# Two transformer blocks on one core: how X is turned for a norm without a mean, and when the low part of a row unit is made

## What is computed

```python
for l in range(2):                                # first block
    x = x + gated_parallel_mixer(rmsnorm(x, norm1_g[l]), ...)
    x = x + conv_ffn(rmsnorm(x, norm2_g[l]), ...)
x = rmsnorm(x, final_g)

# second block
x = layer_norm(alpha * x + rwkv_moba_mixer(x), ln1_g[0], ln1_b[0])
x = layer_norm(alpha * x + sq_relu_mlp(x), ln2_g[0], ln2_b[0])
x = layer_norm(alpha * x + dilated_mixer(x), ln1_g[1], ln1_b[1])
x = layer_norm(alpha * x + sq_relu_mlp(x), ln2_g[1], ln2_b[1])

def rmsnorm(x, g):                                # a norm without a mean
    return x * rsqrt(mean(x * x) + 1e-6) * g
```

## Time and profile before

| what | value |
|---|---|
| median of 3 runs | 1582.14 us (1581.43 to 1585.51) |
| the profiled execution, its time | 1585.99 us |
| its span, first to last instruction | 1584.2 us |
| mean granted TensorE clock | 0.997 |
| TensorE busy | 1554.5 us, 98% |
| VectorE busy | 1089.2 us, 69% |
| ScalarE busy | 930.4 us, 59% |
| GpSimd busy | 303.2 us, 19% |
| HBM read | 269.88 MB, 171 GB/s over the span |

### The profile page before, as it was taken

One profiled execution on the slowest core, in us unless ns is written; L12 is line 12 of the kernel. 1 busy time (PEld: TensorE's weight loads), 2 busy tenths in 40 slices (PEclk: granted clock), 3 DMA queues, 4 the chain that ended last, 5 costly groups with the idle time before them and its releaser, 6 DMA issues. The chain is left out here.

```text
span 1584.2 us, 29408 instructions
## 1 busy us (share of the span) xinstructions
PE 1554.5 (98%) x12262; PEld 1424.6 (90%) x12262; DVE 1089.2 (69%) x1702; ACT 930.4 (59%) x1507; POOL 303.2 (19%) x214
## 2 busy tenths in 40 slices
PE   9999999999999999999999999899999999999998
PEld 7999998999899999999988997779988899889986
DVE  5775666887457765668864587679744778789644
ACT  6787756665457776566654664345433666664431
POOL 0000210443000002104420352018500021118300
PEclk9999999999999999999999999999999999999999
DMA  8344455565552534636554631235555535345651
GB/s 331 123 150 144 146 201 186 192 238 197 197 181 92 174 123 157 225 134 213 200 186 173 242 120 55 83 127 193 203 213 196 191 131 187 107 186 192 238 203 59
DMA packets 42324, 272.82 MB, mean 172 GB/s; under 512 B 4816, under 2 KB 4944, under 8 KB 13392
## 3 DMA queue, kind: packets, MB, share of 16 engines
q1 hardware_dynamic: 41184, 265.18, 47.0%
q10 hardware_dynamic: 1008, 5.77, 1.0%
HBM read 269.88 MB, written 1.05 MB: 171 GB/s over the span
## 5 line engine op out<-in xcount | busy, mean ns | idle before, releaser
L330 DVE TENSOR_TENSOR b_wlo<-b_wraw,b_whi 128x2048 fp32r<-128x2048 f32 (+3 forms) x261 | 564.1, 2165 | 178.4 <-PE b_ps L466 126.7
L403 PE MATMUL b_ps<-b_H,b_whi 128*128 128x256 f32 x2152 | 604.8, 281 | 0.5 <-DVE b_trot L796 0.5
L406 PE MATMUL b_ps<-b_H,b_wlo 128*128 128x256 f32 x2152 | 598.1, 278 | 0.0
L405 PE MATMUL b_ps<-b_H,b_whi 128*128 128x256 f32 x2152 | 598.0, 278 | 0.0
L322 ACT ACTIVATE b_whi<-b_wraw 128x2048 fp32r<-128x2048 f32 (+3 forms) x262 | 466.6, 1782 | 205.2 <-PE b_ps L466 149.1
L403 PEld LDWEIGHTS b_ps<-b_H,b_whi 128*128 128x128 f32 x2152 | 404.8, 188 | 8.7 <-issue 6.8
L405 PEld LDWEIGHTS b_ps<-b_H,b_whi 128*128 128x128 f32 x2152 | 406.1, 189 | 0.7
L406 PEld LDWEIGHTS b_ps<-b_H,b_wlo 128*128 128x128 f32 x2152 | 406.0, 189 | 0.0
L1596 POOL TENSOR_TENSOR b_fl<-b_ab,b_fh 128x256 fp32r<-128x256 f32 x44 | 93.8, 2131 | 205.7 <-ACT b_fh L1569 205.7
L1517 POOL TENSOR_TENSOR b_mg<-b_mg,b_scr 128x256 f32<-128x256 f32 x32 | 31.5, 984 | 405.9 <-DVE b_scr L1502 405.9
L463 PE MATMUL b_ps<-b_whi,b_gh 128*128 128x512 f32 x256 | 99.7, 389 | 0.0
(11 more groups left out here) (361 smaller groups left out, 2464.5 us busy)
## 6 DMA issues: line engine op xcount, KB each, us to landing
b_wraw<-in_w SPq DMA_DIRECT2D x221, 1024.0 KB, 4.8
b_wraw<-in_w SPq DMA_DIRECT2D x35, 512.0 KB, 3.4
b_wraw<-in_w SPq DMA_DIRECT2D x6, 768.0 KB, 5.9
b_bias<-in_rpb SPq DMA_DIRECT2D x8, 512.0 KB, 6.4
b_gains<-in_gains ACTq DMA_DIRECT2D x4, 1024.0 KB, 4.8
b_X<-in_x ACTq DMA_DIRECT2D x2, 512.0 KB, 5.4
b_cA<-in_cA SPq DMA_DIRECT2D x2, 512.0 KB, 6.0
out<-b_X SPq DMA_DIRECT2D x4, 256.0 KB, 2.2
```

Of the source, the lines that this page charges most:

```text
L330: e.tensor_tensor(wlo[u % NLO][:, 0:n], raw[u % NRAW][:, 0:n], hi.bitcast(F32), ALU.subtract).then_inc(up("w_lo", "wlo", u))
L403: e.matmul(out, wh, x.hi[:, kk, :], start=k == 0, stop=False)
L405: e.matmul(out, wh, x.lo[:, kk, :], start=False, stop=False)
L406: ins = e.matmul(out, wl, x.hi[:, kk, :], start=False, stop=last)
```

## The change

First, in the four norms without a mean that follow a product (not `n10`, whose kind is now called "first"), the diagonal is no longer made. VectorE writes half 0 of the block of X times `rinv` to a buffer, ScalarE half 1 to a second one, and TensorE transposes these copies with the identity. The buffers are `S_ring[0]` and `S_ring[1]` of the mixer and the two halves of `rows` of the ffn; there is one pair for both token blocks, so block 1's copies wait until block 0's transposes have read them. X stays as it is.

Second, at the last block of every stage end but the final one (seven places), the low part of unit `last + 2` is made by two instructions of 1024 columns, one ahead of the sum into X and one behind it. TensorE's first two k of that unit wait for the first half only, the third k for the second.

The diff, without the places that only hand the buffers on:

```diff
+    def split_lo_in_two(e, w, u, i):
+        a, b = i * UNIT // 2, (i + 1) * UNIT // 2
+        w.wait_ge(*at("whi", u))
+        w.wait_ge(*at("unit", u - NLO))
+        ins = e.tensor_tensor(wlo[u % NLO][:, a:b], raw[u % NRAW][:, a:b], whi[u % NHI][:, a:b].bitcast(F32), ALU.subtract)
+        if i == 0:
+            ins.then_inc(up("w_first_lo", "wlo", "half", u))
+        else:
             ins.then_inc(up("w_lo", "wlo", u))
             w.unit = u + 1
...
-    def row_pe(e, w, job, j, pi, tb, q0=0, q1=None, ring="lin"):
+    def row_pe(e, w, job, j, pi, tb, q0=0, q1=None, ring="lin", in_two=False):
...
-        w.wait_ge(*(at("wlo", u) if u > 1 else at("wlo", "half", u)))
+        in_two = in_two or u < 2
+        w.wait_ge(*(at("wlo", "half", u) if in_two else at("wlo", u)))
         for q in range(q0, q1):
             k = ks[q]
-            if u < 2 and q == 2:
+            if in_two and q == 2:
                 w.wait_ge(*at("wlo", u))
...
             if n == 2 and key != "n10":
-                turn_x_pe(e, w, key, kind, 1)
-            row_pe(e, w, job, *b)
+                turn_x_pe(e, w, key, kind, 1, xs)
+            row_pe(e, w, job, *b, in_two=b[1] == 1)
...
+    def rms_scale_dve(e, w, key, tb, xs):
+        s = tst[:, tb, :]
+        w.wait_ge(*at(key, "root", tb))
+        e.reciprocal(s[:, 4:5], s[:, 3:4]).then_inc(up("x_rinv", key, "rinv", tb))
+        w.wait_ge(*at(key, "rinv", tb))
+        if tb:
+            w.wait_ge(*at("full", ("xt", key, 0, 1)))
+        e.tensor_scalar(xs[0], x_half(0, tb), s[:, 4:5], None, ALU.mult).then_inc(up("x_n", key, "xn", 0, tb))
+
+    def rms_scale_act(e, w, key, tb, xs):
+        w.wait_ge(*at(key, "rinv", tb))
+        if tb:
+            w.wait_ge(*at("full", ("xt", key, 0, 3)))
+        e.activation(xs[1], x_half(1, tb), ACT.Copy, scale=tst[:, tb, 4:5]).then_inc(up("x_n_act", key, "xn", 1, tb))
...
-    def turn_x_pe(e, w, key, kind, tb):
+    def turn_x_pe(e, w, key, kind, tb, xs=None):
...
-                if kind == "rms":
+                if kind == "first":
                     w.wait_ge(*at(key, "diag", tb))
                     ins = e.matmul(out, x, diag[:, tb, :], start=True, stop=True)
                 else:
                     w.wait_ge(*at(key, "xn", f // 4, tb))
-                    ins = e.transpose(out, x, ident)
+                    ins = e.transpose(out, x if xs is None else xs[f // 4][:, f % 4 * P:f % 4 * P + P], ident)
...
             if kind == "rms":
                 rms_sum_act(e, w, key, j, tb, ("free", (job.key, j, tb)))
+                if j == 1:
+                    rms_scale_act(e, w, key, tb, xs)
...
         for n, (j, tb) in enumerate(row_done(job)):
-            ahead_to(e, w, split_lo, begun[(job.key, 0)][-1] + AHEAD_LO if n < 2 and len(begun[(job.key, 0)]) > 1 else last + AHEAD_LO if n == 3 else last - 1 + AHEAD_LO)
+            in_two = n == 3 and kind != "last"
+            ahead_to(e, w, split_lo, begun[(job.key, 0)][-1] + AHEAD_LO if n < 2 and len(begun[(job.key, 0)]) > 1 else last + AHEAD_LO if n == 3 and not in_two else last - 1 + AHEAD_LO)
+            if in_two:
+                split_lo_in_two(e, w, last + AHEAD_LO, 0)
             ahead = kind == "ln" and single(job)
             if not (ahead and (j, tb) == (0, 1)):
                 res_dve(e, w, job, j, tb, scale, need)
+                if in_two:
+                    split_lo_in_two(e, w, last + AHEAD_LO, 1)
                 if kind != "rms":
                     ln_stats_dve(e, w, key, j, tb, ("free", (job.key, j, tb)))
             if j == 1:
                 if kind == "rms":
-                    rms_diag_dve(e, w, key, tb)
+                    rms_scale_dve(e, w, key, tb, xs)
...
+                self.scaled = [S_ring[0][:, :], S_ring[1][:, :]]
...
+                self.scaled = [self.rows[:, 0, :], self.rows[:, 1, :]]
...
         for tb in range(2):
-            turn_x_pe(e, w, "n10", "rms", tb)
+            turn_x_pe(e, w, "n10", "first", tb)
```

More of the change, by code:

```diff
@@ L340, in split_lo_half @@
             w.unit = u + 1
+    def split_lo_in_two(e, w, u, i):
[6 more added lines that the diff above has]
+        else:
+            ins.then_inc(up("w_lo", "wlo", u))
+            w.unit = u + 1
     def half_act(e, w, u, i):
@@ L474, in row_pe, with first_rows_pe @@
             ins.then_inc(up("part", "unit", u))
-    def first_rows_pe(e, w, job, key, kind):
+    def first_rows_pe(e, w, job, key, kind, xs=None):
         blocks = row_blocks(job)
@@ L721, in single, with end_pe @@
         return job.nk <= job.kpart
-    def end_pe(e, w, job, key, kind):
+    def end_pe(e, w, job, key, kind, xs=None):
         blocks = row_blocks(job)
@@ L730, in end_pe, with end_act @@
         if kind != "last":
-            turn_x_pe(e, w, key, kind, 0)
+            turn_x_pe(e, w, key, kind, 0, xs)
         row_pe(e, w, job, *blocks[-1], q)
-    def end_act(e, w, job, key, kind, gkey=None, bkey=None):
+    def end_act(e, w, job, key, kind, gkey=None, bkey=None, xs=None):
         last = last_unit(job)
@@ L747, in end_act, with end_dve @@
                 h_act(e, w, key, gkey, bkey, tb)
-    def end_dve(e, w, job, key, kind, gkey, bkey, scale, need=None):
+    def end_dve(e, w, job, key, kind, gkey, bkey, scale, need=None, xs=None):
         last = last_unit(job)
         for n, (j, tb) in enumerate(row_done(job)):
-            ahead_to(e, w, split_lo, begun[(job.key, 0)][-1] + AHEAD_LO if n < 2 and len(begun[(job.key, 0)]) > 1 else last + AHEAD_LO if n == 3 else last - 1 + AHEAD_LO)
+            in_two = n == 3 and kind != "last"
+            ahead_to(e, w, split_lo, begun[(job.key, 0)][-1] + AHEAD_LO if n < 2 and len(begun[(job.key, 0)]) > 1 else last + AHEAD_LO if n == 3 and not in_two else last - 1 + AHEAD_LO)
+            if in_two:
+                split_lo_in_two(e, w, last + AHEAD_LO, 0)
             ahead = kind == "ln" and single(job)
@@ L1314, in pe @@
             banks.assign(lin=EVERY, att=EVERY)
-            first_rows_pe(e, w, self.v, f"n1{self.l}", "rms")
+            first_rows_pe(e, w, self.v, f"n1{self.l}", "rms", ffns[self.l - 1].scaled if self.l else None)
             for j in range(4):
@@ L1358, in pe @@
                 tile_pe(e, w, self.gates[br] if what == "gate" else self.brs[br], j)
-            end_pe(e, w, self.out, f"n2{self.l}", "rms")
+            end_pe(e, w, self.out, f"n2{self.l}", "rms", self.scaled)
         def act(self, e, w):
@@ L1408, in act @@
                 self.branch_act(e, w, what, *i)
-            end_act(e, w, self.out, f"n2{l}", "rms", f"norm2_g{l}")
+            end_act(e, w, self.out, f"n2{l}", "rms", f"norm2_g{l}", xs=self.scaled)
         def bias_sp(self, e, w, rq):
@@ L1486, in dve @@
                 self.branch_dve(e, w, what, *i)
-            end_dve(e, w, self.out, f"n2{l}", "rms", f"norm2_g{l}", None, 1.0)
+            end_dve(e, w, self.out, f"n2{l}", "rms", f"norm2_g{l}", None, 1.0, xs=self.scaled)
         def branch_dve(self, e, w, what, br, j):
@@ L1540, in pe @@
             banks.assign(lin=EVERY, att=EVERY)
-            first_rows_pe(e, w, self.first, f"n2{self.l}", "rms")
+            first_rows_pe(e, w, self.first, f"n2{self.l}", "rms", mixers[self.l].scaled)
             for m in self.order:
@@ L1547, in pe @@
                         tile_pe(e, w, self.up_, 2 * m + g)
-            end_pe(e, w, self.down, self.next[0], "rms")
+            end_pe(e, w, self.down, self.next[0], "rms", self.scaled)
         def act(self, e, w):
@@ L1569, in act @@
                     e.activation(self.f.hi[:, m, :], A[:, 0, :], ACT.Copy).then_inc(up("f_hi", k, "hi", m))
-            end_act(e, w, self.down, self.next[0], "rms", self.next[1])
+            end_act(e, w, self.down, self.next[0], "rms", self.next[1], xs=self.scaled)
         def dve(self, e, w):
@@ L1590, in dve @@
                     e.tensor_tensor(A[:, 0, :], A[:, 0, :], A[:, 1, :], ALU.mult).then_inc(up("gated", "gated", l, m))
-            end_dve(e, w, self.down, self.next[0], "rms", self.next[1], None, 1.0)
+            end_dve(e, w, self.down, self.next[0], "rms", self.next[1], None, 1.0, xs=self.scaled)
         def pool(self, e, w):
@@ L2210, in pe @@
             banks.assign(lin=ALL, att=ALL)
-            first_rows_pe(e, w, self.v, "nf", "rms")
+            first_rows_pe(e, w, self.v, "nf", "rms", ffns[1].scaled)
             for what, i in self.steps[:7]:
```

## The result

The changed kernel took 1591.43 us (median of seven runs, 1585.85 to 1592.42), the kernel before beside it 1582.36 (seven runs, 1581.43 to 1587.84): 1.0043 times as long over all runs, interval 1.0029 to 1.0056 (the two medians alone would give 1.0057). The forecast, 1578.7 with a range up to 1583.0, was wrong, and in sign. The profiled execution took 1587.07 us, with a span of 1585.3; that of before 1585.99 and 1584.2.

What follows compares the result with a forecast made beforehand. TensorE, busy 98% of the span, was taken as the bound. Two `down` ends (0.71 + 0.17 each) and two mixer ends (0.73 + 0.17 each), less 0.15, gave 3.4 us off 1582.14: 1578.7, range 1574.6 to 1583.0.

Steps and rivals of the forecast that it cites:

- Part 1: Turning X by transposes, not the diagonal: 0.80 us to the next row product against 1.70, 0.90 less TensorE each.
- The clock rival: Slower: transposes let TensorE's clock drop, row products behind the eight turnings take double, 22 us, 1600; chance 0.03.
- Part 2: First turnings wait for VectorE's scaled half of X, costing 0.17 us each; the four save 2.9 us.
- Part 3: H of block 0 behind the first turning comes at the same time as before, with no wait for TensorE.
- part 4: Low part in two: 0.38 us wait gone, new 0.4 us wait; 0.71 gained at `down` ends, 0.73 at mixers'.
- Part 5: Second turnings: TensorE then waits for H, so only 0.17 of 0.90 us is kept, four times, 0.7 us.
- The first rival: Second turnings pay in full because H comes quicker: bound 7.3 us gained, 1574.8; chance 0.20.
- Part 6: Three norms with a mean: the low-part wait moves to the second half and the turning; 0.15 us lost in sum.
- The Sum: Whole kernel: the local terms come to 3.4 us, taken off the median 1582.14 for a forecast of 1578.7.
- The second rival: Almost nothing gained: ScalarE's copy late at first turnings, or a later chain takes the gain back; 1.1 us, 1581.0; chance 0.16.
- the slower rivals: Two: ScalarE's copy behind its own split at turnings, 1588.9, chance 0.04; clock lowered by transposes, 1600, chance 0.03.

Runs made afterwards that it cites:

- e3: Kernel before with only the low part made in two, turning still by the diagonal: 1581.08 us, 1.0000 of the kernel before.
- e2: Changed kernel with the low part left whole, so the turnings by transposes alone: 1584.41 us, 1.0022 of the kernel before.
- e1: Changed kernel run again with no edit: 1588.58 us, 1.0044 of the kernel before; its profiled execution took 1591.15 us.
- e5: Changed kernel with block 1 (second turning) turned by the diagonal again: 1589.68 us, 1.0015 of the kernel before.
- e6: Changed kernel with only the second turning by transposes, block 0 by the diagonal, low part whole: 1591.46 us, 1.0027 of the kernel before.
- e7: Changed kernel with two overwritten identity products ahead of each stretch of 912 products: 1588.10 us, 1.0000 of the kernel before.
- e8: Changed kernel with the second turning three products earlier in norms without a mean: 1586.35 us, 0.9992 of the kernel before.
- e11: The kernel of e8 once more, on another chip: 1586.36 us, 0.9991 of the kernel before.
- e9: Changed kernel with an overwritten pair of 128- and 256-column products ahead of the four long stretches: 1589.12 us, 1.0011 of the kernel before.
- e13: Changed kernel with the second and third matmul of each tile product swapped: 1582.73 us, 1.0003 of the kernel before.

## Why the prediction was wrong, by its own steps

**Part 1** held: 434.93 - 434.11 = 0.82 us from the turning to the next row product, forecast 0.80. The clock rival fell: busy time of after by stretch, behind a first and a second turning by transposes,

```profile
434.00:438.00 4.00, 4.00 (x22) 3.38 (x22) 2.33 (x8) 3.64 (x10) 0.00 (x0) 1.00 0.03 6
442.50:446.50 4.00, 3.76 (x20) 2.82 (x19) 2.45 (x9) 3.56 (x10) 0.24 (x1) 1.00 0.60 246
```

both at 1.00, the upper level (2.4 GHz). The Trainium skill says in "TensorE: Matmul & The Clock Gate", "PE-mode transpose", that a transpose doesn't count as TensorE being busy in the same way, from which the rival took its lower clock; behind these eight no trace shows one.

**Part 2** held. TensorE could start the first turning at 433.77 + 0.23 = 434.00 and started at 434.11: a hold of 0.11, forecast 0.17. The copies into other buffers were a little cheaper than those in place (0.49 and 0.72 against 0.54 and 0.82).

**Part 3** held, and **part 4** in what it comes to. The halves start 1.73 us apart, around a sum at +1.14, as worked out; the wait in between is 441.03 less the due 440.55 + 0.23, so 0.25 us, forecast 0.4. A `down` end was to last 9.33 - 0.71 - 0.17 = 8.45 from turning to turning and lasted 8.41; a mixer's 10.04 - 0.73 - 0.17 = 9.14 and lasted 9.16. One reading in it was wrong. The bracket of 0.38 us at 442.50 counts from the end of the matmul before, but the next would have started before that end: the one before started at 441.73, so the next was due at 441.96 and lost 0.54 us. The row ahead of it in the timeline of before:

```profile
441.73 0.39 PE L466 MATMUL b_ps<-b_whi,b_H 128*128 128x512 f32 x1
```

With the 0.1 behind it that is the 0.65 us that the split alone gained in e3, where 0.38 was expected at each `down` end. It also leaves a wait where part 4 had none: in after the first product of the second unit was due at 438.92 + 0.23 and started at 439.29, 0.14 us late:

```profile
438.92 0.39 PE L478 MATMUL b_ps<-b_whi,b_H 128*128 128x512 f32 x1
...
439.29 0.50 PE L475 MATMUL b_ps<-b_whi,b_H 128*128 128x512 f32 x1
```

The sum isn't touched, since the second half of the low part sets the time there. And the parts don't need each other at `down` ends: from 9.33, e2 gained 0.22 and e3 0.65, both together 0.93, so they simply add.

**Part 5** held, a little low. The third product stands 444.44 - 442.52 = 1.92 us behind the second turning, forecast 2.07: the first gain starts 0.42 us into the turning where the sum had 0.48, and VectorE's two instructions reached TensorE in 0.66 and not 0.75. The fourth product stands 2.25 us behind it, where it stood 2.48, so 0.23 and not 0.17 of the 0.90 is kept. The first rival, that second turnings pay in full, fell.

**Part 6** had the mechanism right and 0.1 us a norm wrong. At `l10` the timeline of after, against the earlier trace rows:

```profile
1050.18 1.22 DVE L346 TENSOR_TENSOR b_wlo<-b_wraw,b_whi 128x1024 fp32r<-128x1024 f32 x1
...
1051.91 1.22 DVE L346 TENSOR_TENSOR b_wlo<-b_wraw,b_whi 128x1024 fp32r<-128x1024 f32 x1
...
1054.68 0.54 DVE L614 TENSOR_SCALAR b_X<-b_X,b_tst 128x512 f32<-128x512 f32 x1
...
1055.37 1.06 PE L634 MATMUL b_ps<-b_c,b_X 128*128 128x128 f32 x8 [0.52 <-DVE b_X L614]
```

The wait for the low part turned into one for L614, but the second turning is 1056.75 - 1055.37 = 1.38 us ahead of before where the way in had 1.31: 0.07 gained and not 0.05 lost. Why the two halves are no dearer than the whole wasn't tried.

**The Sum is the step that failed.** Its terms come to 4.06 + 0.17 = 4.2 us where I had 3.4; what failed is the last line, in which the local gain is taken off the time of the whole, the rest counted as unchanged. 6.7 us came back in that rest: 0.65 and 2.79 as pitch in two stretches, and 3.21 in the rest of the rwkv layer. There after shows two falls of the clock and before one, and 1.3 us goes where the second falls; the other 1.9 goes in steps where TensorE pauses for "issue" (0.63, 1.67, 0.82 and 0.67 in after, against 1.90 in before). With the 1.05 of the start on the other side, -1.05 - 4.2 + 6.7 comes to +1.4, where the spans differ by 1.1; the 0.3 left is spread over the other stages. The second rival names "a later chain" but prices it as the loss of a gain; it allows for no loss, and chains weren't the cause. Of the slower rivals, one needed ScalarE's copy to be late and the other a clock lowered by transposes; neither occurred. The range was too narrow for the same reason. Its upper edge took the 4.1 us between three runs for the scatter, where four long stretches with two pitches (2 x 4.2 and 2 x 2.8) and the recurrence (some 3) can move one execution by 17 us; before itself ran from 1579.8 to 1595.4 on the second chip. (The lower edge, 1574.6, should be the first rival's 1574.8; nothing hangs on it.)

The pair of profiles doesn't show all of the loss of the medians, 9.07 us: after's profiled execution is the second shortest of its seven. e1 shows what a run of that length can hold, both ffn stretches at 117.8.

**Does the change itself bring the longer pitch?** Shown is that the time lost stands in unchanged stretches, that one program runs there at either pitch, and that placement changes the pitch. Not shown is that the change raises the odds. For it: of the long ffn stretches (the traces at the kernel's own placement, both product orders), those of kernels that turn the second block by the diagonal ran at the longer pitch 3 times in 12, those by transposes 15 in 22; the difference times 8.4 us for two stretches is (0.68 - 0.25) x 8.4 = 3.6 us, about the local gain. Two of the three are e5's, which turns the first block by transposes; without any such turning it is 1 in 10, with one 17 in 24. The two first comparisons gave the same loss, 1.0043 and 1.0044, and e2 and e6, with transposes and no split, lie clear above 1 as well, where e3, the split alone, doesn't. Against: the two stretches of an execution mostly go together, so by executions with at least one at the longer pitch it is 2 in 6 against 8 in 11; the other kernels with transposes (e5, e7, e8 and e11, e9, e13) don't differ from before by more than their intervals; and the changed kernel itself gave 1.0000 and 0.9998 on two other chips. Each chip was used on one occasion, so chip and occasion can't be told apart. What picks the pitch stays open.

No kernel tried is faster than before by more than its interval. The nearest is the early second turning (e8, e11), 0.9992 and 0.9991 on two chips.

## To carry to other kernels

Put two traces beside each other instruction by instruction: that shows in one table that a change did what it was meant to, and where, far off, the time went. Before a gain of 0.2% is forecast for a whole kernel, look at how long one unchanged instruction lasts in the longest stretches of several executions: if it has two values, their difference times their count is the error bar of the forecast, and one chip and one profile settle nothing below it. A local sum can be right to 0.2 us a place and still not show in the measured time. And count a wait of pipelined matmuls from the start that was due, not from the end of the one before.

## What the runs showed of the hardware

- The same comparison came out differently: the changed kernel against before was 1.0043, 1.0044, 1.0000 and 0.9998, the last three on three different chips.
